# A hybrid diffusion trunk step: the second sub-layer's order of work, modulation pairs inside attention, projections between the scan levels, and one level pass in thirds

## What is computed

```
a_q, a_ff, a_fb, a_i, a_g, b_q, b_k, b_v = split(h @ ab_w_in)          # 8 parts of 512 columns
f = lb + (1 - lb) * sigmoid(z);  k = (1 - lb) * sigmoid(-z)            # z = a_ff forward, a_fb backward
scan over tokens, forward and backward: S = f * S + k v^T;  o = q S     # 4 heads of 128 x 128
o_a = rmsnorm(o_fwd + o_bwd, gnorm) * silu(a_g)
o_b = softmax(q k^T / 8 (+ relative bias, window, cached context)) v    # 8 heads of 64
out = concat(o_a, o_b) @ ab_w_out
```

## Time and profile before

| what | value |
|---|---|
| runs | 1732.07, 1732.15, 1733.76 us; median 1732.15 |
| the profiled execution | 1731.67 us; its span 1729.8 us |
| mean granted TensorE clock | 0.974 of full |
| busy: PE, PEld | 1654.7 us (96%), 1612.7 us (93%) |
| busy: DVE, ACT, POOL | 826.1 us (48%), 677.3 us (39%), 85.0 us (5%) |
| chain that ended last | PE 87%, DVE 7%, issue 2%, DMA 2%, ACT 1% |
| DMA | 260.54 MB, mean 151 GB/s |

### The profile page before, as it was taken

The page is one execution under the profiler, slowest core; times in us unless marked ns, Lnnn a source line. Parts: engine busy times, 40 slices in busy tenths (PEclk is TensorE's granted clock), DMA queues, the critical chain, the costliest instruction groups (busy, mean ns, idle before and its releaser), DMA issues.

```text
span 1729.8 us, 28048 instructions
## 1 busy us (share of the span) xinstructions
PE 1654.7 (96%) x11541; PEld 1612.7 (93%) x11541; DVE 826.1 (48%) x1276; ACT 677.3 (39%) x1174; POOL 85.0 (5%) x68
## 2 busy tenths in 40 slices
PE   4999999998997899999999999999999999999997
PEld 3999999998886889899999999999989998999997
DVE  1544434563434768644334644343463676444333
ACT  2533333353334025533334453333454265333332
POOL 2000000010111340000000000000000000000000
PEclk8999999999998799999999999999999999999998
DMA  9643366673447662633333634336454366333310
GB/s 332 196 133 121 121 207 214 218 209 91 105 87 255 200 204 80 195 122 122 129 120 121 197 128 132 121 122 201 141 171 145 99 220 196 122 121 117 122 54 37
DMA packets 255921, 260.54 MB, mean 151 GB/s; under 512 B 6625, under 2 KB 253826, under 8 KB 255826
## 3 DMA queue, kind: packets, MB, share of 16 engines
q1 hardware_dynamic: 249664, 251.67, 44.8%
q0 software_dynamic: 1184, 3.11, 1.9%
q10 hardware_dynamic: 4978, 4.41, 0.8%
HBM read 256.56 MB, written 2.62 MB: 150 GB/s over the span
## 4 chain that ended last, share of the span: by engine, by line
PE 87%; DVE 7%; issue 2%; DMA 2%; ACT 1%; SPq 0%; DVEq 0%; ACTq 0%
PE bank L395 24%; PE bank L396 23%; PE bank L397 23%; PE bank L1382 3%; PE bank L1649 2%; DMA RAW<-in_mod_w 2%; DVE X L1003 1%; DVE HL L969 1%; PE bank L1405 1%; PE bank L1610 1%; DVE OUTF L999 1%; PE bank L1542 1%; PE bank L418 1%; PE bank L417 1%; PE bank L416 1%
## 5 line engine op out<-in xcount | busy, mean ns | idle before, releaser
L362 DVE TENSOR_TENSOR WL<-RAW,WH 128x1024 fp32r<-128x1024 f32 (+1 forms) x331 | 398.8, 1206 | 726.4 <-ACT WH L348 726.0
L348 ACT ACTIVATE WH<-RAW 128x1024 fp32r<-128x1024 f32 (+1 forms) x344 | 358.3, 1045 | 690.7 <-PE bank L397 662.8
L395 PE MATMUL bank<-HH,WH 128*128 128x384 f32 x1664 | 562.7, 338 | 2.2 <-ACT MIX L648 2.2
L396 PE MATMUL bank<-HL,WH 128*128 128x384 f32 x1664 | 560.3, 337 | 0.0
L397 PE MATMUL bank<-HH,WL 128*128 128x384 f32 x1664 | 560.2, 337 | 0.0
L395 PEld LDWEIGHTS bank<-HH,WH 128*128 128x128 f32 x1664 | 313.8, 189 | 5.2 <-ACT MIX L648 2.6
L396 PEld LDWEIGHTS bank<-HL,WH 128*128 128x128 f32 x1664 | 313.7, 189 | 0.0
L397 PEld LDWEIGHTS bank<-HH,WL 128*128 128x128 f32 x1664 | 313.7, 189 | 0.0
L395 PE MATMUL bank<-AH,WH 128*128 128x384 f32 x704 | 237.3, 337 | 0.0
L396 PE MATMUL bank<-AL,WH 128*128 128x384 f32 x704 | 236.6, 336 | 0.0
L397 PE MATMUL bank<-AH,WL 128*128 128x384 f32 x704 | 236.6, 336 | 0.0
(11 more groups left out here) (212 smaller groups left out, 1503.9 us busy)
## 6 DMA issues: line engine op xcount, KB each, us to landing
RAW<-in_ffn_w_in SPq DMA_DIRECT2D x88, 1024.0 KB, 5.1
RAW<-in_mod_w SPq DMA_DIRECT2D x72, 1024.0 KB, 5.8
RAW<-in_ffn_w_out SPq DMA_DIRECT2D x32, 1024.0 KB, 5.1
RAW<-in_ab_w_in SPq DMA_DIRECT2D x16, 1024.0 KB, 6.0
RAW<-in_ffn_w_out SPq DMA_DIRECT2D x16, 768.0 KB, 5.3
RAW<-in_cv_w_in SPq DMA_DIRECT2D x12, 1024.0 KB, 5.2
RAW<-in_ab_w_out SPq DMA_DIRECT2D x4, 1024.0 KB, 7.2
RAW<-in_cv_w_out SPq DMA_DIRECT2D x4, 1024.0 KB, 6.8
```

The lines of the kernel that those rows point to most:

```text
L348: e.activation(WH[:, (2 * m + b) % 4, 0:nk, :], RAW[:, p, 0:nk, b * P:(b + 1) * P], ACT.Copy).then_inc(half_hi, 1)
L362: e.tensor_tensor(WL[:, k, 0:nk, :], RAW[:, p, 0:nk, b * P:(b + 1) * P], WH[:, k, 0:nk, :].bitcast(F32), ALU.subtract).then_inc(half_ready, 1)
L395: e.matmul(out, WH[:, k, kk, :], xh(kk), start=(first and kk == 0), stop=False)
L396: e.matmul(out, WH[:, k, kk, :], xl(kk), start=False, stop=False)
```

## The change

The second sub-layer is ordered anew; the arithmetic stays.

- Context keys are turned after `tau` 5, and the keys for the output after `tau` 8 (bank 7). Keys and values have a semaphore each for their store.
- In attention every even step has one projection, `tau` 12 to 23: FF, FB and then the queries (`AB_ORDER` changes so). Every odd step has one modulation pair of group C, so that all twelve lie in attention; every fourth step turns a group. The six groups all have bank 3. `ring_order` follows.
- The sigmoids of a direction stand on ScalarE after steps 7 and 15, its gate arithmetic on VectorE in steps 9 to 11 and 17 to 19. GpSimd no longer scales KFW.
- The product with the values takes the two latent blocks of a head in one matmul of 256 columns.
- V (`tau` 24 to 27) and G (28 to 31) are projected one `tau` before the levels and one after each level. G leaves PSUM through Silu on ScalarE.
- A level is one pass: forward and backward are joined. ScalarE copies the left halves of KFW and the right halves of KBW into KJ (`join`), and one matmul per unit of 128 columns takes queries that alternate between QB and QF in the same way. The work is in thirds of four units and 512 words: a third has four matmuls, one masked copy and one query update on VectorE, one key update on GpSimd and one totals instruction on VectorE. The masked copy writes whole rows with a mask of 128 columns.
- VectorE does the four splits of the last two projection tiles in levels 1 to 4. ScalarE's splits for the output projection go with the projections of G.

The core of the diff:

```diff
-MOD_BANK = [7, 6, 7, 3, 2, 6, 3, 2, 3, 7, 2, 7, 6, 6, 7, 6, 0, 6]
+MOD_BANK = [7, 6, 7, 3, 2, 6, 3, 3, 3, 3, 3, 3, 6, 6, 7, 6, 0, 6]
...
+        if kind == "even":
+            order += run(f"in{s}", 2, 9)
+            for q in range(6):
+                order += run("modC", 4 * q, 4 * q + 4) + (run(f"in{s}", 9 + q, 10 + q) if q < 5 else [])
+            order += run(f"in{s}", 14, 16)
...
-        AB_ORDER = [10, 11, 12, 13, 14, 15, 0, 1, 6, 7, 2, 3, 4, 5, 8, 9]
+        AB_ORDER = [10, 11, 12, 13, 14, 15, 2, 3, 4, 5, 0, 1, 6, 7, 8, 9]
...
+        def two_halves(t, other, at, blocks, b, left=0, right=None):
+
+            a, z = t.rearrange("p h n -> p (h n)"), other.rearrange("p h n -> p (h n)")
+            step = z.offset - a.offset + (b if right is None else right) - left
+            return bass.AP(tensor=a.tensor, offset=a.offset + at + left, ap=[a.ap[0], [2 * b, blocks], [step, 2], [1, b]])
...
             for lv in range(LEVELS):
                 b = 1 << lv
-                for w in range(2):
-                    pool.wait_ge(lvl_mm, 2 * lv + w + 1)
...
+                for j in range(3):
+                    pool.wait_ge(k_joined, 3 * lv + j + 1)
+                    if lv:
+                        pool.wait_ge(lvl_t, 3 * (lv - 1) + j + 1)
+                    else:
+                        pool.wait_ge(ks_done, j + 1)
+                        pool.wait_ge(q_gated, j + 1)
+                    k = two_halves(KFW, KBW, 512 * j, 256 // b, b)
+                    pool.tensor_tensor(k, k, two_totals(FF, FB, 512 * j, 256 // b, b, b, 0, b),
+                                       ALU.mult).then_inc(lvl_k, 1)
...
+                    if part == 4:
+                        act.wait_ge(half_used, used(f"in{s}", tau // 2, tau % 2))
+                        act.wait_ge(diag_mm, 3)
+                        act.activation(G[:, q, :], cols3(B), ACT.Silu).then_inc(proj_out, 1)
+                        halves_ahead[tau % 2]()
+                        return
...
+                def gate_sigmoids(w):
+
+                    z, k = (FF, FB)[w], (KFW, KBW)[w]
+                    act.wait_ge(proj_out, 16 + 4 * w)
+                    act.activation(k, z, ACT.Sigmoid, scale=-1.0).then_inc(sig_done, 1)
+                    act.wait_ge(sig_done, 2 * w + 1)
+                    act.activation(z, z, ACT.Sigmoid).then_inc(sig_done, 1)
...
+                    if step % 4 == 1 and step > 1:
+                        mod_cols_out(g0 + step // 4 - 1)
...
+                    if step % 4 == 0 and step > 0:
+                        mod_rows_out(g0 + step // 4 - 1)
+                    if step < 24 and step % 2 == 0:
+                        proj(12 + step // 2)
+                    if step in (7, 15):
+                        gate_sigmoids(step // 8)
+
+                def join(lv):
+
+                    b = 1 << lv
+                    for j in range(3):
+                        if lv:
+                            act.wait_ge(lvl_mm, 3 * (lv - 1) + j + 1)
+                            act.wait_ge(lvl_k, 3 * (lv - 1) + j + 1)
+                        act.activation(KJ[:, 512 * j:512 * j + 512].rearrange("p (m w i) -> p m w i", w=2, i=b),
+                                       two_halves(KFW, KBW, 512 * j, 256 // b, b), ACT.Copy).then_inc(k_joined, 1)
+
+                act.wait_ge(prep, 18)
+                for lv in range(LEVELS):
+                    join(lv)
+                    proj(24 + lv)
+                proj(31)
...
                 for lv in range(LEVELS):
                     b = 1 << lv
...
+                    for j in range(3):
+                        dve.wait_ge(lvl_mm, 3 * lv + j + 1)
                         if lv == 0:
...
+                            dve.wait_ge(diag_out, j + 1)
+                        else:
+                            dve.wait_ge(lvl_out, 3 * (lv - 1) + j + 1)
+                            dve.wait_ge(lvl_t, 3 * (lv - 1) + j + 1)
+                        mask = LMASK[:, lv:lv + 1, :].broadcast_to([P, 4, P])
+                        dve.copy_predicated(ATT[:, 4 * j:4 * j + 4, :], mask,
+                                            bank[j][:].rearrange("p (u t) -> p u t", u=4)).then_inc(lvl_out, 1)
...
+                        q = two_halves(QB, QF, 512 * j, 256 // b, b)
+                        dve.tensor_tensor(q, q, two_totals(FB, FF, 512 * j, 256 // b, b, b, 0, b),
+                                          ALU.mult).then_inc(lvl_q, 1)
+                        if j:
+                            totals(lv, j - 1)
+                    if 1 <= lv <= 4:
+                        split_dve(dve, f"in{s}", 14 + (lv - 1) // 2, 8)[(lv - 1) % 2]()
+                    totals(lv, 2)
...
+                proj(24)
                 for lv in range(LEVELS):
                     b = 1 << lv
...
+                    for j in range(3):
                         if lv == 0:
...
+                            pe.wait_ge(diag_out, j + 1)
+                            pe.wait_ge(q_gated, j + 1)
                         else:
...
+                            pe.wait_ge(lvl_out, 3 * (lv - 1) + j + 1)
+                            pe.wait_ge(lvl_q, 3 * (lv - 1) + j + 1)
+                        pe.wait_ge(k_joined, 3 * lv + j + 1)
+                        for u in range(4 * j, 4 * j + 4):
+                            mm = pe.matmul(bank[j][:, (u % 4) * P:(u % 4 + 1) * P],
+                                           KJ[:, P * u:P * u + P],
+                                           two_halves(QB, QF, P * u, 64 // b, b), start=True, stop=True)
                         mm.then_inc(lvl_mm, 1)
...
+                    proj(25 + lv)
```

More of the change, by code:

```diff
@@ L765, in even @@
                         act.wait_ge(p_turned, u + 1)
+                        if u == 0:
+                            act.wait_ge(k_stored, 16)
                         if u >= 2:
@@ L1108, in proj_low, with tick, gate, clamp @@
                                           ALU.subtract).then_inc(proj_lo, 1)
+                ticks = [0]
+                def tick(x):
+                    x.then_inc(prep, 1)
+                    ticks[0] += 1
+                def gate(t, w, k=False):
+                    for h in range(HEADS_A):
+                        lb, one_less = LBT[:, 2, 4 * w + h:4 * w + h + 1], LBT[:, 3, 4 * w + h:4 * w + h + 1]
+                        if k:
+                            tick(dve.tensor_scalar(t[:, h, :], t[:, h, :], one_less, None, ALU.mult))
+                        else:
+                            tick(dve.tensor_scalar(t[:, h, :], t[:, h, :], one_less, lb, ALU.mult, ALU.add))
+                def clamp(t):
+                    dve.wait_ge(prep, ticks[0])
+                    tick(dve.tensor_scalar(t, t, 1e-30, None, ALU.max))
+                g0 = first_group("modC")
                 for tau in range(12):
@@ L1115, in even @@
                         coefficients(between(s))
[L1116 to L1119 removed]
+                    if tau == 7:
+                        dve.wait_ge(ctx_ready, 1)
+                        dve.tensor_tensor(BKL[:, :, DEC_SEQ:NT], bank[6][:].rearrange("p (a b) -> p a b", a=4),
+                                          BKH[:, :, DEC_SEQ:NT].bitcast(F32), ALU.subtract).then_inc(ctx_lo, 1)
+                for step in range(24 + 1):
                     u = step
@@ new lines, in even @@
+                    if step in (10, 18):
+                        gate((KFW, KBW)[step // 8 - 1], step // 8 - 1, k=True)
+                    if step in (11, 19):
+                        clamp((FF, FB)[step // 8 - 1])
+                    if step % 4 == 2 and 6 <= step < 26:
+                        coefficients(g0 + step // 4 - 1)
+                assert ticks[0] == 18, ticks
+                dve.wait_ge(prep, 18)
+                dve.wait_ge(s_mm, 24)
+                flat = lambda t, j: t.rearrange("p h n -> p (h n)")[:, 512 * j:512 * j + 512]
@@ L1192, in cat_lo @@
+                coefficients(g0 + 5)
                 def cat_lo(ht):
@@ L1195, in cat_lo, with totals @@
                                       ALU.subtract).then_inc(cat_ready, 1)
-                meanwhile = [silu_g] + [lambda ht=ht: cat_lo(ht) for ht in range(4)]
-                assert n[0] == PREP, n
+                def totals(lv, j):
+                    b = 1 << lv
+                    dve.wait_ge(lvl_k, 3 * lv + j + 1)
+                    dve.wait_ge(lvl_q, 3 * lv + j + 1)
+                    left, right = (two_totals(FF, FB, 512 * j, 256 // b, b, at, at, 1) for at in (0, b))
+                    dve.tensor_tensor(left, left, right, ALU.mult).then_inc(lvl_t, 1)
```

317 lines of the change are left out of this document (120 added, 197 removed).

## The result

| what | before | after |
|---|---|---|
| median of the runs of this comparison | 1732.37 us (4) | 1717.46 us (4; 1714.98 to 1719.40) |
| ratio, 95% interval | | 0.9912 [0.9894, 0.9929] |
| the profiled execution; its span | 1731.67; 1729.8 us | 1719.40; 1717.3 us |
| mean granted clock | 0.974 | 0.974 |
| output projection starts | 650.1 | 632.6 |

The account below looks back on a forecast made before the run. TensorE alone was taken to bound attention, with idle and half-clock time elsewhere; afterwards VectorE would bound the levels. The stages moved the output projection from 650.1 to 624.6, 25.5 us off 1731.67: forecast 1706, range 1686 to 1722.

Parts of the forecast that it names:

- rival A: The forecast itself: waits in attention and VectorE-bound levels as estimated, 1697 to 1715 us; chance 0.47.
- C: Attention's short steps starve: late weights or half clock add 15 us, or 128-column matmuls cost double, 1721 us; chance 0.17.
- Step 1: Before attention: context and key transposes go ahead, the 4.9 us hole goes, attention starts at 400.5 instead of 404.4, full clock.
- Step 2: Attention: 120 us of TensorE work plus 17 us of waits (bounds 6 and 28), five of 1.8 us for the column copy.
- Step 3: Sigmoids inside attention: 5.5 us on ScalarE each time with table load, nothing on the path.
- Step 4: Weight loads in attention: 230 GB/s against 350 reached, hidden by about 3 us; the 5.0 us weight wait goes.
- Step 5: Clock in attention: half clock behind short gaps costs 2 us, bounds 0 and 17; attention ends at 539.5.
- step 7: Levels on TensorE: matmuls of 128 columns take half, 2.8 us a level, seven save 19.6; 49 us with V and G.
- Step 8: Levels on VectorE: rounds of 11.6 to 6.4 us, 57 us against TensorE's 49; VectorE the bound, ending at 605.
- Step 9: State and output: 3.4 us, then 16.2 us as before; output projection starts at 624.6.
- B: TensorE hides all: VectorE's level round under 7 us, attention's chain costs 8 us, not 17; 1689 us; chance 0.25.
- D: Operands alternating between two tensors run at half rate on all engines, six level rounds grow 30 us; 1736, slower; chance 0.07.

Follow-up runs that it names:

- Run 6: The changed kernel with the context-key transposes and their copies put back behind the last value projection, as before the change; 1724.04 us, ratio 0.9944.
- Run 1: The changed kernel with ScalarE copying the modulation columns ahead of the same step's exponential in attention instead of behind it; 1705.70 us, ratio 0.9843.
- run 8: The changed kernel with the edits of run 1, run 2, run 7 and run 4 together; 1690.15 us, ratio 0.9744.
- run 9: The kernel of run 8 with the sigmoids and VectorE's gate arithmetic two steps later in attention; 1689.39 us, ratio 0.9738.
- run 3: The changed kernel without GpSimd's 21 key updates in the levels, so scan outputs and states differ; 1711.52 us, ratio 0.9875.
- run 2: The changed kernel with VectorE's weight split in attention moved to the odd step, behind its maximum and scaling; 1709.84 us, ratio 0.9858.
- run 7: The kernel of run 2 with five projection tiles loaded in attention two places later in the ring; 1696.33 us, ratio 0.9781.
- run 4: The changed kernel with ScalarE's casts of attention's output behind the turned-key copies and VectorE's low parts behind the state updates; 1711.65 us, ratio 0.9878.
- run 5: The changed kernel with the 21 key updates of the levels on VectorE, ahead of the totals, instead of on GpSimd; 1721.66 us, ratio 0.9928.

## Why the forecast was right, and where it was mis-sized

The sign and the new bounds came out as the prediction put them; the gain was 15 us where 26 were forecast. The time, 1717.5, is above the 1697 to 1715 that rival A had for itself, and the sign named for C, a clock under 0.95 in attention, came (0.92). The stated range held because it took in C. In the profiled execution the output projection starts 8.0 us later than the forecast 624.6, and the rest takes 5.0 us longer than before.

- **Step 1, context ahead.** First scores at 402.1, forecast 400.5: 1.6 us late, no wait before them, within the scatter of 400.2 to 403.8 over the runs. Run 6 brings the hole back: 7.3 us by its own lines, forecast 7.3.
- **Step 2, work and waits of attention.** Waits 19.6 us, forecast 17, bounds 6 and 28. The column copy was forecast as five waits of 1.8 us, 9 in all; it is five, 8.0. Run 1 takes them away and shows the cause. Waits for the transposes reach 2.6 us each and not 0.1 to 0.7; how much of them is the gate arithmetic no run separates. Work: at clock 0.99 run 8 is busy 113.4 us from unit 1 on and 4.8 before, 118.2 in all, of which the clock is at most 1.2. So the work is 117 to 118 us, where the prices gave 120. Most of that is the merged product, taken at nothing: its six records take 1.51 us at full clock where two old units took 0.87 each, so a head pays 0.2 us less.
- **Step 3, sigmoids.** The table load has no idle time behind it, as forecast: in run 8 the load at 440.89 takes 1.28 us and the exponential starts at 442.19. But "nothing on the path" failed. From the first table load on ScalarE works without a gap up to the row copy, and TensorE's turn waits for that copy, 1.0 us behind the first pair of sigmoids and 2.2 behind the second. ScalarE, then TensorE, after:

```profile
492.49 1.28 ACT L761 ACT_TABLE_LOAD   x1
```
```profile
499.48 0.61 PE L1425 MATMUL bank<-IDENT,ROWS 128*128 128x8 f32 x4 [2.17 <-ACT ROWS L604]
```

  With the exponential earlier (run 8) they are 0.4 and 0.6 us, and with the sigmoids moved too (run 9) they are gone.
- **Step 4, weights.** In the profiled execution they are hidden, with no wait for RAW; in the repeat of the same kernel one of 2.4 us stands, and in run 3 one of 2.2. The margin of "some 3 us" was as thin as said or thinner: run 2 makes VectorE's release later and 12.1 us of waits for weights appear. The 350 GB/s that the prediction set against its 230 were not to be had in attention: there the DMA engines are busy 0.97 of the time at 265 GB/s (run 8), 1.10 at 350 in the earlier trace rows.
- **Step 5, the clock: this is the term that was mis-sized.** The prediction took 2 us between bounds of 0 and 17. Attention has a mean clock of 0.92, by which up to 11.7 us are lost (8% of 146.7); from the busy time, 127.0 against the 117 to 118 of step 2, it is 9 to 10 us, 7 to 8 more than forecast. Half clock stands behind many of the waits of 1 to 3 us, which come back every few steps; the single 1.2 us gap that left the clock at 1.00 was the wrong row to lean on, since it was alone. When the waits shrink, so does the loss: clock 0.94, 0.97 and 0.99 in runs 1, 7 and 8. It does not follow the waits alone: with nearly the same waits it was 0.92, 0.90 and 0.89 (after, repeated, run 4), and run 9 has 0.95 with the idle time of run 8.
- **Step 6, diagonal.** From the first diagonal matmul to level 0 8.8 us, forecast 8.6.
- **Step 7, levels on TensorE.** 168 records, as forecast, 22.9 us of busy time against 19.6. Half of the difference is levels 0 and 1, which the last section shows. The choice of "half" came out, but one reason for it was misread: a projection of 4.4 us is 24 matmuls of 384 columns and not 72, so 0.18 us each, little below the 0.23 of a level matmul.
- **Step 8, levels on VectorE.** VectorE is the bound, as forecast; run 3 takes GpSimd away and TensorE becomes it. TensorE's waits are 3.7 us in four pieces, put down to issue, fewer than the one a round that was forecast. The first masked copies of the levels start at the times of these lines (after, the first and the last; 568.29, 578.03, 586.43, 593.93 and 601.13 lie between):

```profile
559.17 0.80 DVE L1249 COPY_PREDICATED MIX<-LMASK,bank 128x512 f32<-128x512 int32 x1 [1.51 <-PE bank L1685]
...
606.30 0.73 DVE L1249 COPY_PREDICATED MIX<-LMASK,bank 128x512 f32<-128x512 int32 x1
```

  Rounds of 9.1, 9.7, 8.4, 7.5, 7.2 and 5.2 us, forecast 11.6, 9.3, 8.2, 7.8, 7.6 and 6.4 (the terms given for the second add up to 9.0). Only the first is far off: GpSimd's updates of level 0 begin before the first masked copy. From level 0 to the end of G 53.9 us, forecast 57.
- **Step 9, state.** 21.1 us from the end of G, forecast 19.6. The terms of the old stage were kept, and four low parts of 8.19 us were not counted. In the kernel before they stood between the levels (2.54 us for the one beside GpSimd, 0.54 to 0.55 for the others, from 581.43 on), and the change puts them behind the levels, beside GpSimd's splits. Run 4 moves them and ScalarE's high parts and gains 5.2 us in this stage; the two are not separated.
- **"Nothing changes behind."** It does, by 5.0 us, with the same instructions. More of it ran at half clock in the kernel after. In the repeat it was 1084.5 again, in the runs 1 to 9 it lay between 1079.7 and 1085.3. Why it goes with one kernel and not with another stays open; the section on the hardware shows a place.
- **The rivals.** Of C, the short steps that starve, the half-clock part took place, 7 to 8 of its 15 us. B, everything hidden, needed the changes of runs 1, 2, 4 and 7; its time, 1689, is what run 8 reaches, which is a coincidence of sums. D fell: updates of 512 without GpSimd beside them take 0.69 us from level 1 on. Of the 13.2 us missing in the profiled execution 8.0 lie before the output and 5.0 in the rest. The 8.0 are: start +1.6, attention +7.7 (waits +2.6, clock +7 to +8, work -2 to -3), diagonal +0.2, levels -3.1, state +1.5. These are differences of stage ends and add up by themselves; they show where the time went, and the causes rest on the runs.

## What to carry to other kernels

When long and short steps alternate, follow the latency from one engine's work to the next and not only the busy sums: a copy of 0.17 us that is ready goes ahead of the instruction that has to wait, and a split that others don't need yet goes behind the chain that they do. Count repeated gaps of 1 to 3 us on TensorE once as gaps and again as half clock; here 19.6 us of gaps came with 9 to 10 us of loss. Before an engine's work is moved later, look at what it releases in an in-order load queue, and let no load that is needed next stand behind one that waits for that release.

## What the runs showed of the hardware that was not expected

**The same gap, two clocks.** The same work behind the output projection, in each kernel with the same two waits of 0.9 and 1.9 us, which end at 1423.6 and 1436.3 after and at 1437.3 and 1450.0 before; first after, then before:

```profile
1425.00:1437.00 12.00, 10.13 (x58) 9.52 (x57) 9.42 (x19) 10.75 (x23) 0.00 (x0) 1.00 0.59 189
1437.00:1450.00 13.00, 13.00 (x69) 13.00 (x68) 8.26 (x11) 7.83 (x13) 0.00 (x0) 0.87 0.49 161
```
```profile
1442.00:1454.00 12.00, 10.13 (x58) 9.69 (x57) 7.64 (x14) 10.89 (x22) 0.00 (x0) 1.00 0.32 101
1454.00:1467.00 13.00, 13.00 (x79) 13.00 (x77) 8.04 (x11) 6.01 (x10) 0.00 (x0) 1.00 0.50 164
```

TensorE was busy 10.13 of 12 us in both; then one went on at full clock, 79 matmuls in 13 us, and the other partly at 1.2 GHz, 69. (The stretches of before stand 3.3 us later in the work; 1450.67 to 1463.67, which matches, is at 1.00 too, with 78.) A gap of this size is followed by half clock in one kernel and not in the other, with the same instructions around it. No experiment here was made on that.

**Alternating operands cost at b = 1 and hardly beyond.** TensorE's 12 matmuls (24 records) at levels 0, 1 and 2, then VectorE's query update at level 0 and at level 2 where GpSimd was not beside it, after:

```profile
557.65 4.15 PE L1685 MATMUL bank<-MIX,TT 128*128 128x128 f32 x24
...
564.46 3.25 PE L1685 MATMUL bank<-MIX,TT 128*128 128x128 f32 x24
...
573.16 2.84 PE L1685 MATMUL bank<-MIX,TT 128*128 128x128 f32 x24
```
```profile
559.85 1.12 DVE L1254 TENSOR_TENSOR MIX<-MIX 128x512 f32<-128x512 f32 x1
...
580.97 0.68 DVE L1254 TENSOR_TENSOR MIX<-MIX 128x512 f32<-128x512 f32 x1
```

In the kernel without key updates the update takes 0.69 us at level 1 already. ScalarE's joins take 0.70 to 0.74 at level 0 and 0.62 to 0.64 later. By the rule of the Trainium skill ("SBUF — State Buffer", "Door 1: The DMA port swizzle") that two hits in a 16-byte line give the full rate, only b = 1 pays; the rows agree, but for 0.2 (run 3) to 0.4 us (after) on TensorE at b = 2. And 128 moved columns cost 2.84 us for 24 records, where 64 cost 5.57 for 48: in this form a matmul costs the same for 64 and for 128 columns, as step 7 took it. That the weights set the price no run shows.

**Sharing with GpSimd.** The same VectorE update took 0.68 us alone and this long beside GpSimd, after:

```profile
578.66 1.76 DVE L1254 TENSOR_TENSOR MIX<-MIX 128x512 f32<-128x512 f32 x1
```

while the masked copy beside it kept its 0.72 to 0.74. In these rows what grew was the instruction with both inputs in SBUF, which also holds for the low parts (8.19 against 2.27 us); the masked copy reads its values from PSUM.
